# First mixer of a two-block kernel: three groups of y are kept, and their output products run two rounds later

## What is computed

```python
def ssd_mixer(u, w_in, conv_w, conv_b, dt_bias, a_log, d_skip, gnorm, w_out):
    z, xbc, dt = split(u @ w_in, [D_INNER, D_INNER + SSD_CONV_DIM])
    xh, bm, cm = split(silu(dwconv(xbc, conv_w, conv_b)), ...)
    dt = softplus(dt + dt_bias)
    a = -exp(a_log)
    y = (ssd_scan(xh, dt[:, :, 0], a[0], bm, cm)
         + rev(ssd_scan(rev(xh), rev(dt[:, :, 1]), a[1], rev(bm), rev(cm)))
         + xh * d_skip[:, None])
    y = y.reshape(bsz, seq, D_INNER) * silu(z)
    y = rmsnorm(y.reshape(bsz, seq, SSD_GROUPS, D_INNER // SSD_GROUPS), gnorm.reshape(SSD_GROUPS, -1))
    return y.reshape(bsz, seq, D_INNER) @ w_out
```

## Time and profile before

| what | us |
|---|---|
| median of 3 runs | 1920.49 (1918.66 to 1925.13) |
| the profiled execution's own time | 1918.41 |
| its span, first to last instruction | 1916.7 |
| round 1 of the mixer | about 62 to 128.0 |
| round 2 | 128.0 to 194.05 |
| round 7 | 457.0 to 522.7 |
| round 8 | 522.7 to 577.7 |
| round 9, to the first product of the next mixer | 577.7 to 609.0 |

### The profile page before, as it was taken

The page is one execution under the profiler, slowest core; times in us unless marked ns, Lnnn a source line. Parts: engine busy times, 40 slices in busy tenths (PEclk is TensorE's granted clock), DMA queues, the critical chain, the costliest instruction groups (busy, mean ns, idle before and its releaser), DMA issues. The chain is left out here.

```text
span 1916.7 us, 21367 instructions
## 1 busy us (share of the span) xinstructions
PE 1764.0 (92%) x8104; PEld 1424.9 (74%) x8104; DVE 1187.6 (62%) x1580; ACT 773.6 (40%) x1140; POOL 405.8 (21%) x351
## 2 busy tenths in 40 slices
PE   5989999999977989999997799999899999999997
PEld 4767787777755767878785577888678778888886
DVE  6768877887866646474744675777565553434343
ACT  5433443344324344444433344445444442323232
POOL 0444743564363000000000601222031020000001
PEclk9989999999988898999997899999999999999999
DMA  3312222222201312222221232222323223333331
GB/s 98 89 43 58 65 66 66 64 63 73 56 24 33 85 50 66 77 66 77 67 77 37 60 88 58 67 69 58 99 88 99 88 79 99 98 91 97 99 99 67
DMA packets 252188, 139.18 MB, mean 73 GB/s; under 512 B 25965, under 2 KB 246550, under 8 KB 252086
## 3 DMA queue, kind: packets, MB, share of 16 engines
q1 hardware_dynamic: 252086, 137.82, 25.3%
HBM read 135.70 MB, written 2.10 MB: 72 GB/s over the span
## 5 line engine op out<-in xcount | busy, mean ns | idle before, releaser
L65 PE MATMUL stream<-u_lo,weights_hi 128*128 128x512 f32 (+2 forms) x1312 | 528.7, 403 | 20.5 <-DVE h L1028 5.0
L67 PE MATMUL stream<-u_hi,weights_hi 128*128 128x512 f32 (+2 forms) x1312 | 516.6, 394 | 0.0
L66 PE MATMUL stream<-u_hi,weights_lo 128*128 128x512 f32 (+2 forms) x1312 | 516.5, 394 | 0.0
L133 DVE TENSOR_TENSOR weights_lo<-weights_raw,weights_hi 128x1024 fp32r<-128x1024 f32 (+4 forms) x266 | 335.7, 1263 | 287.1 <-ACT weights_hi L123 287.0
L123 ACT ACTIVATE weights_hi<-weights_raw 128x1024 fp32r<-128x1024 f32 (+4 forms) x266 | 268.4, 1010 | 487.8 <-PE stream L67 455.3
L65 PEld LDWEIGHTS stream<-u_lo,weights_hi 128*128 128x128 f32 (+2 forms) x1312 | 249.7, 190 | 87.3 <-issue 18.9
L66 PEld LDWEIGHTS stream<-u_hi,weights_lo 128*128 128x128 f32 (+2 forms) x1312 | 249.3, 190 | 53.9 <-issue 2.7
L67 PEld LDWEIGHTS stream<-u_hi,weights_hi 128*128 128x128 f32 (+2 forms) x1312 | 248.4, 189 | 55.0 <-issue 0.2
L203 POOL COPY h_sum_of_squares<-h_squares 128x512 f32<-128x512 f32 x5 | 3.2, 649 | 829.0 <-ACT h_squares L191 829.0
L65 PE MATMUL stream<-mlp_a_lo,weights_hi 128*128 128x512 f32 x256 | 100.2, 391 | 0.0
L67 PE MATMUL stream<-mlp_a_hi,weights_hi 128*128 128x512 f32 x256 | 99.7, 389 | 0.0
(11 more groups left out here) (472 smaller groups left out, 3185.2 us busy)
## 6 DMA issues: line engine op xcount, KB each, us to landing
weights_raw<-in_w_mlp_dram SPq DMA_DIRECT2D x64, 512.0 KB, 4.0
weights_raw<-in_ssd_w_in_dram SPq DMA_DIRECT2D x48, 512.0 KB, 3.9
weights_raw<-in_gla_w_in_dram SPq DMA_DIRECT2D x40, 512.0 KB, 3.7
weights_raw<-in_w_in_dram SPq DMA_DIRECT2D x29, 512.0 KB, 3.7
weights_raw<-in_ssd_w_out_dram SPq DMA_DIRECT2D x16, 512.0 KB, 3.7
weights_raw<-in_gla_w_out_dram SPq DMA_DIRECT2D x16, 512.0 KB, 3.3
weights_raw<-in_w_out_dram SPq DMA_DIRECT2D x8, 512.0 KB, 3.8
weights_raw<-in_w_xkv_dram SPq DMA_DIRECT2D x8, 512.0 KB, 4.0
```

The costliest lines, as they stand in the source:

```text
L65: pe.matmul(out, lh, rl, start=first, stop=False, skip_group_check=skip)
L66: pe.matmul(out, ll, rh, start=False, stop=False, skip_group_check=skip)
L67: return pe.matmul(out, lh, rh, start=False, stop=last, skip_group_check=skip)
L133: dve.tensor_tensor(lo, raw_view(c, n), hi.bitcast(F32), ALU.subtract).then_inc(c.w_split, 1)
```

## The change

The y_hi and y_lo buffers hold three groups (`SSD_Y`, `kept`). The output units of groups 0 to 3 run two rounds later than before (rounds 4 to 7, slots 4 and 7). Those of groups 4 and 5 run in round 8, slots 2, 3, 4 and 6; those of group 6 in round 9, slots 0 and 2; those of group 7 in round 9, slots 4 and 7, as before. Rounds 2 and 3 have no output units. The work buffer also holds dt, la and cum of the stage's start, to make room. The conditions for the conv steps name the rounds that have conv inputs, as output units now stand in conv slots of round 8.

```diff
 SSD_SLOTS = 8
 SSD_ROUNDS = SG + 2
-SSD_AT = {(g, half): (g + 2, 4 + 3 * half) for g in range(SG) for half in range(2)}
-SSD_AT[SG - 2, 1] = (SG + 1, 0)
+SSD_Y = 3
+SSD_AT = {(g, half): (g + 1 + SSD_Y, 4 + 3 * half) for g in range(SG - 1 - SSD_Y) for half in range(2)}
+SSD_AT.update({(SG - 4, 0): (SG, 2), (SG - 4, 1): (SG, 3), (SG - 3, 0): (SG, 4), (SG - 3, 1): (SG, 6),
+               (SG - 2, 0): (SG + 1, 0), (SG - 2, 1): (SG + 1, 2),
+               (SG - 1, 0): (SG + 1, 4), (SG - 1, 1): (SG + 1, 7)})
...
-        dt, la, cum = sb("dt", [64, T]), sb("la", [64, T]), sb("cum", [64, T])
+        work = sb("work", [P, 3, T])
+        dt, la, cum = (work[0:64, j, :] for j in range(3))
...
-        work = mb("work", [P, 3, T])
...
-        yh, yl = mb("y_hi", [P, 2, T], F32R), mb("y_lo", [P, 2, T], F32R)
+        yh, yl = mb("y_hi", [P, 2 * SSD_Y, T], F32R), mb("y_lo", [P, 2 * SSD_Y, T], F32R)
+        kept = lambda f: slice(2 * (f % SSD_Y), 2 * (f % SSD_Y) + 2)
...
-                            pe.wait_ge(s_yl, SSD_OUT[i, k][0] + 1)
-                            stream_products(c, pe, n, lambda j: yh[:, j, :], lambda j: yl[:, j, :])
+                            e = SSD_OUT[i, k][0]
+                            pe.wait_ge(s_yl, e + 1)
+                            stream_products(c, pe, n, lambda j: yh[:, kept(e), :][:, j, :],
+                                            lambda j: yl[:, kept(e), :][:, j, :])
...
-                    if (pi, pk) in plan and pk in CONV:
+                    if pi in G and pk in CONV:
...
-                        if f:
-                            act.wait_ge(c.tile_done, c.tiles_before[plan[SSD_AT[f - 1, 1]] + 1])
-                        act.activation(yh[:, :, :], y[:, :, :], ACT.Copy).then_inc(s_yh, 1)
+                        if f >= SSD_Y:
+                            act.wait_ge(c.tile_done, c.tiles_before[plan[SSD_AT[f - SSD_Y, 1]] + 1])
+                        act.activation(yh[:, kept(f), :], y[:, :, :], ACT.Copy).then_inc(s_yh, 1)
...
-                        dve.tensor_tensor(yl[:, :, :], y[:, :, :], yh[:, :, :].bitcast(F32), ALU.subtract)\
+                        dve.tensor_tensor(yl[:, kept(f), :], y[:, :, :], yh[:, kept(f), :].bitcast(F32), ALU.subtract)\
```

## The result

The median of 20 runs is 1924.34 us (1922.18 to 1929.6) against 1917.2 us for before, also 20 runs; the ratio is 1.0038, 95% interval 1.003 to 1.0047, so 7.1 us or 0.38% slower. The forecast was 8.7 us slower, and 1929.2 us in all; 3.3 of the 4.9 us between 1929.2 and 1924.3 are those by which before's median of 3 runs, 1920.49, lay above that of 20. The profiled execution has a span of 1920.5 us.

What follows compares the result with a forecast made beforehand. Full rounds keep PE busy, but DVE was taken as the pace of emptied slots, with half clock behind waits. -1.4 + 11.2 - 1.1 = +8.7 us on the 1920.49 us median gives 1929.2 us; range 1917 to 1936.

Steps and rivals of the forecast that it cites:

- Rounds 2 and 3, -1.4 us: Emptied slots 4 and 7: DVE's chain and half clock nearly replace the units, -0.7 us a round; bounds 0 and -12.
- Round 8, +11.2 us: Units put into slots 2, 3 and 6 lengthen round 8 by 11.2 us; bounds +5 and +15.
- Slots 2 and 3: Round 8, each given a unit: slot 2 +0.5 us, slot 3 +5.4 us with a bank wait and half clock.
- the bank wait: Round 8, slot 3: PE waits 3.6 us for an h addition queued on DVE behind slot 2's work; bounds 1 and 5.
- Slots 4 and 5: Round 8: one unit before and after, DVE's extra h additions lie beside it; 0 us, bounds -2 and +1.5.
- Slots 6 and 7: Round 8: the unit in front of y_inter(0) is covered by nothing; +5.3 us, bounds +4 and +6.5.
- Round 9, -1.1 us: Slot 2's unit lies under the chain to y_lo, +0.4 and +0.6; last two units avoid half clock, -2.1; bounds +1, -3.
- leaving the half clock out: Omitting the clock term would make rounds 2 and 3 gain some 4 us more and the filled rounds cost less.
- Shorter waits: Rival, chance 0.24: rounds 2 and 3 give 3 us each, round 8 costs 9; +2 us, 1922.4.
- That the emptied rounds shorten: Rival, chance 0.12: PE's work paces rounds 2 and 3, which lose all four units, 22 us; -11.9 us, 1908.6.
- The rule of interleaving stretches with different bounds: Skill's rule to interleave stretches whose most-contended engine differs; by it, the emptied rounds really shorten, rival's chance 0.12.
- That two output units in a row serialise with DVE: Rival, chance 0.10: in every slot of round 8, slots 4 and 6 waiting 3 us each too; +15 us, 1935.

Runs made afterwards that it cites:

- buffers alone: The kernel after with the output units back in the slots of before, only the buffer layout kept; ratio to before 0.9993 (0.998 to 1.0005).
- busy matmuls: The kernel after with unread matmuls in PE's waits of rounds 2 and 3 (19 in slot 4, 12 in slot 7); ratio to before 1.0019 (1.0006 to 1.0032).
- four units left out: The kernel before without the four output units of groups 0 and 1 in rounds 2 and 3; ratio to before 0.9992 (0.9977 to 1.0007), -1.5 us.
- before, two taps: The kernel before with two of the four conv taps of rounds 2 and 3 left out on DVE; ratio 0.9989 (0.9979 to 1.0), -2.1 us.
- after, two taps: The kernel after with two of the four conv taps of rounds 2 and 3 left out on DVE; ratio to before 1.0006 (0.9994 to 1.0018).

## Why round 8 costs ten microseconds

First suspect: the wait for the bank in slot 3. The h additions of tiles 1 to 3 were put ahead of the normalisation:

```diff
+                    if (i, k) == (NI - 2, 2):
+                        for j in range(1, 4):
+                            close(i, k, j)
                     if k == 2 and f in G:
                         dve.wait_ge(s_rs, 2 * f + 2)
```

(and left out in slot 3).

> The kernel after with the h additions of tiles 1 to 3 of round 8's slot 2 placed ahead of the normalisation of group 6 on DVE. My theory: the wait for the bank (2.9 us) and the half clock behind it (some 2.9 us in the slot 3 unit) go, less a wait for m of slot 3 of 1 to 1.5 us that comes back: 4 to 5 us faster than the kernel after, so 2 to 3 us slower than before. Rival: the serial steps of round 8 are the pace anyway, then under 1 us faster than the kernel after.

Measured: 1.0045 (1.0028 to 1.0062), no faster than the kernel after. My theory fell. PE and DVE of this kernel:

```profile
547.92 0.39 PE L65 MATMUL stream<-ssd_y_lo,weights_hi 128*128 128x512 f32 x1
...
554.27 0.80 PE L65 MATMUL stream<-ssd_y_lo,weights_hi 128*128 128x512 f32 x1 [2.08 <-DVE h L1034]
```

```profile
545.46 1.87 DVE L1034 TENSOR_TENSOR h<-h,stream 128x512 f32<-128x512 f32 x3
...
549.78 1.85 DVE L1177 TENSOR_TENSOR ssd_y_lo<-ssd_y,ssd_y_hi 128x1024 fp32r<-128x1024 f32 x1 [1.13 <-ACT ssd_y_hi L1008]
551.56 2.06 DVE L133 TENSOR_TENSOR weights_lo<-weights_raw,weights_hi 128x1024 fp32r<-128x1024 f32 x1
553.54 0.68 DVE L1034 TENSOR_TENSOR h<-h,stream 128x512 f32<-128x512 f32 x1
```

The first tile of slot 3 no longer waits, the fourth does: it needs the h addition of the first, which stands behind the same y_lo and a split. The queue of DVE in slot 2 is as long as before, and what PE needs next stands behind it whichever addition goes first. Slots 2 and 3 take 20.2 us instead of 22.3 (539.77 to 559.99); round 8 is 64.2 us long, 1.2 less, and 2.4 more are lost in round 9 (33.9 against 31.6), where PE waits 2.07 us for h in slot 0 (0.48 in the kernel after) and then runs the norm's products at half clock (3.78 us against 1.98). That this comes from the edit isn't shown: in this profile rounds 2 to 4, where the two programs are the same, also take 1.7 us more (198.4 against 196.7).

Second: is it the number of units or their slots? The unit of slot 6 moved to slot 7:

```diff
-               (SG - 3, 1): (SG, 6),
+               (SG - 3, 1): (SG, 7),
```

> The kernel after with one of the four units of round 8 in another slot: the second unit of group 5 in slot 7 instead of slot 6. Theory: it isn't the number of units in round 8 that costs but where they stand. In slot 6 nothing covers the unit (5.5 us); in slot 7 it lies beside the chain conv or h additions, exponential, assemble, y_inter(1), as in the full rounds, where a slot 7 with a unit lasts 9.2 us and one without 8.8 to 8.9. So 4 to 5 us faster than the kernel after, 2 to 3 us slower than before. Rival: DVE's h additions make the round as long wherever the unit stands: within 1.5 us of the kernel after.

Measured: 1.0016 (1.0005 to 1.0027), 4.2 us less than the kernel after, as expected.

```profile
572.42 1.96 PE L851 MATMUL q<-ssd_bc,ssd_state 128*128 128x128 f32 x12
...
574.44 0.39 PE L65 MATMUL stream<-ssd_y_lo,weights_hi 128*128 128x512 f32 x1
...
581.72 0.40 PE L65 MATMUL stream<-ssd_y_lo,weights_hi 128*128 128x512 f32 x1
```

From y_inter(0), at 572.42, to round 9 it is 9.3 us with a unit in it, against 8.3 without one in before: 1.0 us for the unit. In slot 6 the same unit cost 4.2.

Then slots 2, 4, 5 and 7:

```diff
-               (SG - 4, 1): (SG, 3), (SG - 3, 0): (SG, 4), (SG - 3, 1): (SG, 6),
+               (SG - 4, 1): (SG, 4), (SG - 3, 0): (SG, 5), (SG - 3, 1): (SG, 7),
```

> The kernel after with round 8's four units in slots 2, 4, 5 and 7 instead of 2, 3, 4 and 6. Slot 5 lies over the wait for m that the kernel after shows there (3.6 us), and the slot 3 unit with its bank wait (2.9 us) and half clock is gone. Theory: slot 3 costs nothing now and slot 5 some 2 us, 3 us less than before this edit, and slot 7 gives 4 to 5 as alone: 7 to 8 us faster than the kernel after, about level with before (0 to 2 us faster). Rival: with only slot 7's gain, 3 us slower than before.

Measured: 1.0011 (1.0001 to 1.0021), 5.2 us less than the kernel after, only 1 us more than slot 7 alone gives, where I had expected 3. In the traces rounds 8 and 9 together are 90.7 us, against 91.4 with slot 7 alone and 96.9 in the kernel after. Slot 3, now empty, is where it went. First DVE, then PE:

```profile
546.77 1.52 DVE L1173 TENSOR_TENSOR ssd_y_lo<-ssd_y,ssd_y_hi 128x1024 fp32r<-128x1024 f32 x1 [1.12 <-ACT ssd_y_hi L1008]
548.21 1.87 DVE L1034 TENSOR_TENSOR h<-h,stream 128x512 f32<-128x512 f32 x3
...
552.95 2.08 PE L820 MATMUL q<-ssd_m,ssd_x_pair 128*128 128x128 f32 x8 [6.01 <-DVE ssd_m L1148]
556.53 0.63 PE L65 MATMUL stream<-ssd_y_lo,weights_hi 128*128 128x512 f32 x1
```

With a unit in slot 2 and none in slot 3, PE waits 6.01 us for m: DVE's slot 2 (split, h addition, m, normalisation, y_lo) and then three h additions stand in front of it. From the start of slot 2 to that of slot 4 it takes 16.05 us with no unit, 18.75 with one (here, 537.78 to 556.53) and 22.3 with two. By these traces DVE's queue sets this stretch; no run shortened that queue to prove it.

## A version that beats both

If slot 2 of round 9 takes a unit for nothing and slot 4 of round 8 is on the path, then only group 6 should be moved, out of round 8:

```diff
-SSD_AT[SG - 2, 1] = (SG + 1, 0)
+SSD_AT.update({(SG - 2, 0): (SG + 1, 0), (SG - 2, 1): (SG + 1, 2)})
```

with the buffers of the change, and all else as before.

> Only group 6 is moved, out of round 8: its two units run in slots 0 and 2 of round 9, all others as in before. Nothing is put into rounds 2, 3 or 8. By the traces, slot 2 of round 9 takes a unit for 0.2 us, since it lies under the chain to y_lo. Slot 4 of round 8 loses its unit (5.5 us at full clock, 6.9 as it ran): if it was on the path, as slots 4 and 5 had no wait in front of it but m's two of 2 to 3 us, the round is 3 to 5 us shorter, and the kernel 3 to 4.5 us faster than before. Rival: the chain of DVE and POOL takes the unit's place as in rounds 2 and 3, then 0 to 1 us faster.

Measured: 0.9969 (0.9955 to 0.9984), -6 us. Rounds 8 and 9:

```profile
520.95:570.80 49.85, 37.81 (x162) 29.28 (x161) 29.58 (x39) 16.77 (x26) 32.72 (x29) 0.83 0.07 22
570.80:603.30 32.50, 27.11 (x102) 19.83 (x100) 24.36 (x31) 15.51 (x25) 12.65 (x10) 0.92 0.20 53
```

55.0 + 31.4 in before, 49.85 + 32.5 here: -4.0 us, inside the 3 to 4.5 that I expected, while the runs say 6 (3.1 to 8.6). A unit in slot 4 of round 8 cost 5 us, one in slot 2 of round 9 costs 1.1.

One unit more, from round 7's slot 7 to round 8's slot 2:

```diff
+... (SG - 3, 1): (SG, 2)
```

> Only group 6 later (slots 0 and 2 of round 9), and also the second unit of group 5 moved from slot 7 of round 7 to slot 2 of round 8. Slot 2 of round 8 took a unit for 0.7 us in the trace of the kernel after, and slot 7 of a full round gives 0.4 us when emptied, so by this 0.3 us slower than the kernel with group 6 alone, 5 to 6 us faster than before. Rival: PE's clock in slots 3 and 4 of round 8 holds, as the wait in slot 2 is filled: then 2 to 3 us faster than that kernel, 8 us faster than before.

Measured: 0.9977 (0.9963 to 0.999), 4.4 us faster than before and not faster than the last one. Its trace has the same 6.01 us wait for m in slot 3: round 7 is 1.4 us shorter, but rounds 8 and 9 take 86.5 us against 82.4. The 0.7 us that I had read for a unit in slot 2 was not its price alone, as the next unit's wait for the bank came right behind it.

Last, unread matmuls in the waits of rounds 1 and 8 of the version with group 6 alone:

```diff
+                    if (i, k) == (1, 4):
+                        busy(c.tiles_before[plan[1, 5]], 19)
+                    if i == NI - 2 and 2 <= k <= 5:
+                        busy(c.tiles_before[plan[NI - 1, 0]], 3 if k == 2 else 8)
...
+                    if i == NI - 2 and 2 <= k <= 4:
+                        busy(c.tiles_before[plan[NI - 1, 0]], 10 if k == 2 else 8)
...
+                        if i in (1, NI - 2):
+                            busy(c.tiles_before[plan[i + 1, 0]], 12 if i == 1 else 6)
```

> Only group 6 later (slots 0 and 2 of round 9), and unread matmuls in PE's waits of round 1 (19 in slot 4, 12 in slot 7) and of round 8 (3 + 10 in slot 2, 8 + 8 in slots 3 and 4, 8 in slot 5, 6 in slot 7). If waiting is what halves the clock and the clock is on the path there: 3 us in round 1 and 3 us in round 8 less than the kernel with only group 6 later, so 9 to 11 us faster than before. Rival: DVE and POOL are the pace, then no faster than that kernel (4 to 6 us faster than before).

Measured: 0.9951 (0.9935 to 0.9966), 9.4 us faster than before, the lowest ratio of all, from 6 runs; the interval overlaps that of the version without. The total was as expected, its parts were not:

```profile
60.00:122.29 62.29, 58.53 (x291) 48.18 (x290) 48.01 (x61) 24.37 (x35) 28.14 (x22) 1.00 0.22 60
518.49:567.98 49.49, 45.32 (x221) 36.19 (x220) 30.43 (x39) 16.76 (x26) 33.44 (x29) 0.97 0.06 22
```

Round 1 ends 3.6 us earlier than in the version without (122.3 against 125.9), though the next round gives 1.2 back (67.5 us against 66.3). Round 8 has a clock of 0.97 instead of 0.83 and is only 0.4 us shorter: there POOL and DVE are the pace, as the rival said, and the clock brings 0.4 us.

## The gap between 9.9 and 7.1 us

> The kernel after once more, unchanged. In its first profile the mixer from round 2 to the next mixer is 490.9 us against 481.0 in before, 9.9 longer, but the median is only 7.1 us longer; its start up to round 2 is 3.0 us shorter and its end 3.1 us shorter. If start and end vary from run to run and the mixer doesn't, this profile has 490 to 492 us in the mixer and its start and end differ by 1 to 3 us from the first. If the change shortens start and end, they come out as in the first profile within 0.5 us.

Measured: 1.0025 (1.0011 to 1.004), 4.8 us slower than before. The mixer is 490.7 us long, from 124.97 to 615.70, as in the first profile. Its start is the same within 0.1 us and its end differs by 1.1, so neither case of the expectation holds alone. The length of the mixer repeats here within 0.2 us, but it isn't steady in every kernel: with the h additions put early, rounds 2 to 4 are 1.7 us longer, as said, with no edit in them.

That the change shortens the start is not shown. Over all profiles of kernels whose round 1 is unchanged, round 2 starts between 124.5 and 128.8 us: the kernel with the buffers alone has 124.5, while those with the busy matmuls and with two taps, whose programs are the change's up to there, have 128.4 and 128.8. Part of this spread is the clock, as the last section shows; the rest stays open.

The baseline has a share in the gap. Here is the mixer of each kernel whose round 1 has no edit, set against before's one profile, beside the ratio of its runs:

| kernel | mixer from round 2, us | against before, us | by the ratio, us |
|---|---|---|---|
| before | 481.0 | | |
| buffers alone | 481.6 | +0.6 | -1.3 |
| four units left out | 480.4 | -0.6 | -1.5 |
| before, two taps | 478.6 | -2.5 | -2.1 |
| after | 490.9 | +9.9 | +7.3 |
| after again | 490.7 | +9.7 | +4.8 |
| after, busy matmuls | 486.9 | +5.9 | +3.6 |
| after, two taps | 483.5 | +2.4 | +1.2 |
| after, additions early | 493.8 | +12.7 | +8.6 |
| after, slot 7 | 485.8 | +4.7 | +3.1 |
| after, slots 2, 4, 5, 7 | 483.8 | +2.8 | +2.1 |
| group 6 later | 477.4 | -3.6 | -6.0 |
| group 6 and one more | 479.9 | -1.2 | -4.4 |

In all but one the trace lies above the ratio, by 0.7 to 4.9 us, also in the kernel with the buffers alone, whose units stand in before's slots. Against that kernel the change is 9.3 us by the traces and 8.6 by the ratios. So some 2 us of the gap look common to all comparisons with before's profile; what makes them stays open.

## Where the prediction was right and wrong

- **Rounds 2 and 3, -1.4 us: the mechanism right, the size half of it in this trace.** It is -0.3 and -0.8 us in the two rounds, +0.3 in round 4, and -0.7 up to the start of round 8 (393.96 against 394.69 us); with the units left out it is -1.4 in the trace and -1.5 by the runs. In round 2 each piece came as read from round 1: y_intra 10.19 us behind the slot 3 stream (forecast 10.15), 16.05 us from there to the end of the slot 6 stream (15.95), 8.91 in slot 7 (8.84), with the wait (4.75), the half clock behind it (0.50) and the wait of y_inter(1) (2.84).
- **Round 8, +11.2 us: right, +10.4.** Slots 2 and 3 cost 6.2 (forecast 5.9), with the bank wait at 2.9 us (3.6) and half clock in the unit behind it. Slots 4 and 5: -0.1 (0). Slots 6 and 7: 4.2 (5.3), a term mis-sized by 1.1: from y_inter(0) to round 9 it takes 6.4 us against 8.3, where the forecast had put only y_inter(0)'s 1.1 us of gain; y_inter(1) gained 0.8 as well (1.93 us against 2.69).
- **Round 9, -1.1 us: the sign was wrong, +0.2.** Three terms make the difference. Up to the norm's products it takes 8.7 us against 7.9, put at nothing in the forecast: slot 0 runs at half clock for longer (its first 18 matmuls start within 5.0 us, 4.3 in before), which takes back what y_inter(1) had gained in round 8. From there to the unit of slot 4 it is 8.5 against 7.2 us, 1.3 more and not 1.0; the wait of 5.23 us for y_lo became 1.05 for the bank. And the last two units, at full clock now as said, give 1.85 and not 2.1: 14.36 us against 16.21. PE still waits 2.23 us for h in them, 2.00 in before. PE in round 9:

```profile
593.06 1.98 PE L880 MATMUL q<-ssd_exp_cum,ones 128*128 128x512 f32 x4 [1.16 <-ACT ssd_exp_cum L978]
594.48 0.79 PE L65 MATMUL stream<-ssd_y_lo,weights_hi 128*128 128x512 f32 x1
...
601.58 0.47 PE L65 MATMUL stream<-ssd_y_lo,weights_hi 128*128 128x512 f32 x1 [1.05 <-DVE h L1034]
...
613.60 0.50 PE L65 MATMUL stream<-ssd_y_lo,weights_hi 128*128 128x512 f32 x1 [2.23 <-DVE h L1034]
...
615.94 0.63 PE L65 MATMUL stream<-u_lo,weights_hi 128*32 128x512 f32 x1
```

- **The sum.** Its terms were off by +0.7, -0.8 and +1.3 us, in part against each other, so 8.7 stands against 9.9 in the trace and 7.1 by the runs. That it lies between the two is partly luck. Two slips in the working: the bounds of rounds 2 and 3 (0 and -12) and of round 8 (+5 and +15) are not those of their terms, which give +1 and -12, and +3.5 and +16.5; and leaving the half clock out would by these terms have made the two rounds gain some 6 us more, not 4. Filling the waits did gain 4, as the next rounds took back the rest.
- **The rivals.** Shorter waits: no, the wait for m came at 4.75 us in both rounds, and the one for the bank well above its low bound. That the emptied rounds shorten was refuted by leaving the units out. The rule of interleaving stretches with different bounds (Trainium skill, Perfetto Trace Analysis, Optimization Strategy) holds here in a narrower form than I weighed it: moving one unit into a covered slot, with group 6, gained 6 us (4.0 in the trace), moving four lost 7. That two output units in a row serialise with DVE was true in slot 3 and cost no more in slot 4.
- **What I had wrong in thought, not in the sum:** I took the bank wait as the cause of slot 3's price. Putting the additions ahead of y_lo moved the wait to the fourth tile. By the traces of these slots with no, one and two units the cause is the length of DVE's queue in slot 2.

## What to carry to other kernels

Before work is taken out of a full stage, look for a place in the trace where the same stage runs without it: here round 1 told that the stage would be as long. Idle time of an engine in a stage isn't room as such; each slot has its own price, from some 1 us (over a chain of other engines) to 5 (in front of it), and the price of a slot depends on what stands in the next one. Moving a single unit by these prices beat moving four. A wait named in the trace may be only the first thing behind a long queue: reordering the queue moves the wait.

## What the runs showed of the hardware that was not expected

The same wait does not always bring the half clock. In round 1 PE waits 1.97 us ahead of the transposes in all fourteen profiles. In five the eight transposes behind it run at full clock (1.09 to 1.10 us), in nine some or all of them at half (1.43 to 1.97). It doesn't go with the program: before has half, the kernel after full, in both of its profiles, and with slot 7's unit moved, a kernel that is the same up to there, it is half again.

```profile
69.77 1.90 PE L889 MATMUL q<-ident,ssd_x 128*128 128x128 f32 x8 [1.97 <-ACT ssd_bc L1009]
```

```profile
68.08 1.09 PE L895 MATMUL q<-ident,ssd_x 128*128 128x128 f32 x8 [1.97 <-ACT ssd_bc L1015]
```

```profile
68.19 1.97 PE L895 MATMUL q<-ident,ssd_x 128*128 128x128 f32 x8 [1.97 <-ACT ssd_bc L1015]
```

This moves the start of round 2. From the unit at 54 to 57 us to round 2 it takes 70.2 us in the four profiles with full clock there and no edit in round 1, and 71.4 to 71.8 in the nine with half. So two profiles of one program can differ here by more than 1 us through the clock alone.
